# The first modulation vectors of a two-block network: all on VectorE, or slice by slice on VectorE and TensorE

## The reference, cut to what matters

```python
c_act = jax.nn.silu(c)
mod = (c_act @ w_ada[l] + b_ada[l])[:, None, :]
sh1, sc1, gt1, sh2, sc2, gt2 = jnp.split(mod, 6, axis=-1)
h = rms_norm(x, g_mix[l]) * (1.0 + sc1) + sh1
x = x + gt1 * token_mix(h, w_in[l], ...)       # first step inside: z = h @ w_in
```

## Time and profile before

| | us |
|---|---|
| runs of the kernel | 2795.12, 2797.88, 2808.26 |
| median | 2797.88 |
| profiled execution: span from first to last instruction | 2800.8 |
| TensorE busy in it | 2691.0 (96%) |
| VectorE busy | 1985.4 (71%) |
| ScalarE busy | 1455.6 (52%) |
| GpSimd busy | 123.4 (4%) |
| mean granted TensorE clock | 0.986 of full speed |

### The profile page before, as it was taken

One profiled execution on the slowest core, in us unless ns is written; L12 is line 12 of the kernel. 1 busy time (PEld: TensorE's weight loads), 2 busy tenths in 40 slices (PEclk: granted clock), 3 DMA queues, 4 the chain that ended last, 5 costly groups with the idle time before them and its releaser, 6 DMA issues.

```text
span 2800.8 us, 45758 instructions
## 1 busy us (share of the span) xinstructions
PE 2691.0 (96%) x15906; PEld 2311.4 (83%) x15906; DVE 1985.4 (71%) x2871; ACT 1455.6 (52%) x2187; POOL 123.4 (4%) x72
## 2 busy tenths in 40 slices
PE   5999899998999989999999999999999999999999
PEld 3866678885999867888799987999877888799987
DVE  7754689996998566653699847899455753699954
ACT  3353478885555246753555525555236753455532
POOL 1532111100000000000000000000000000000000
PEclk9999799998999999999999999999999999999999
DMA  7631499993332231123233232322232123223222
GB/s 284 273 135 38 169 345 408 406 367 121 106 105 91 90 144 67 52 76 113 83 106 105 90 113 83 104 103 94 90 112 99 60 68 113 98 91 105 90 98 98
DMA packets 95244, 377.57 MB, mean 135 GB/s; under 512 B 10832, under 2 KB 11104, under 8 KB 92896
## 3 DMA queue, kind: packets, MB, share of 16 engines
q1 hardware_dynamic: 89072, 348.69, 34.5%
q0 software_dynamic: 4608, 16.78, 1.5%
q10 hardware_dynamic: 1456, 10.66, 0.9%
HBM read 363.50 MB, written 16.78 MB: 136 GB/s over the span
## 4 chain that ended last, share of the span: by engine, by line
PE 83%; DVE 7%; issue 5%; ACT 4%; DMA 0%; POOL 0%; SPq 0%; ACTq 0%; DVEq 0%; POOLq 0%
PE pb L1402 15%; PE pb L1404 15%; PE pb L1403 15%; PE pb L1787 10%; PE pb L1789 10%; PE pb L1788 10%; PE pb L1971 1%; PE pb L2003 1%; PE pb L1927 1%; PE pb L1476 1%; DVE g_wl L2507 1%; ACT SP L1284 1%; DVE hid L2686 1%; PE pb L1655 1%; PE pb L1980 0%
## 5 line engine op out<-in xcount | busy, mean ns | idle before, releaser
L1787 PE MATMUL pb<-bl,g_wh 128*128 128x256 f32 x2464 | 701.7, 285 | 14.7 <-DVE bl L2597 5.7
L1789 PE MATMUL pb<-bh,g_wh 128*128 128x256 f32 x2464 | 697.9, 283 | 0.0
L1788 PE MATMUL pb<-bh,g_wl 128*128 128x256 f32 x2464 | 697.9, 283 | 0.0
L1787 PEld LDWEIGHTS pb<-bl,g_wh 128*128 128x128 f32 x2464 | 473.5, 192 | 20.1 <-issue 8.4
L1788 PEld LDWEIGHTS pb<-bh,g_wl 128*128 128x128 f32 x2464 | 473.7, 192 | 1.6 <-issue 1.4
L1789 PEld LDWEIGHTS pb<-bh,g_wh 128*128 128x128 f32 x2464 | 473.6, 192 | 0.0
L2636 DVE TENSOR_TENSOR w_lo<-raw,w_hi 128x1024 fp32r<-128x1024 f32 x164 | 200.3, 1223 | 203.1 <-ACT w_hi L679 202.3
L1402 PE MATMUL pb<-hl,w_hi 128*128 128x512 f32 (+1 forms) x728 | 303.1, 416 | 23.4 <-DVE hl L2131 10.2
L679 ACT ACTIVATE w_hi<-raw 128x1024 fp32r<-128x1024 f32 x194 | 204.2, 1057 | 195.2 <-PE pb L1404 181.6
L1404 PE MATMUL pb<-hh,w_hi 128*128 128x512 f32 (+1 forms) x728 | 286.0, 393 | 0.0
L1403 PE MATMUL pb<-hh,w_lo 128*128 128x512 f32 (+1 forms) x728 | 285.9, 393 | 0.0
(11 more groups left out here) (450 smaller groups left out, 5364.1 us busy)
## 6 DMA issues: line engine op xcount, KB each, us to landing
raw<-in_wstream SPq DMA_DIRECT2D x220, 512.0 KB, 3.2
m_raw<-in_moe_stream SPq DMA_DIRECT2D x96, 512.0 KB, 6.0
g_own<-in_gu_stream SPq DMA_DIRECT2D x44, 768.0 KB, 4.0
raw<-in_gu_stream SPq DMA_DIRECT2D x44, 768.0 KB, 4.1
m_first<-in_moe_stream SPq DMA_DIRECT2D x48, 512.0 KB, 6.0
hf<-in_moe_stream SPq DMA_DIRECT2D x48, 512.0 KB
ada_ring<-in_ada SPq DMA_DIRECT2D x8, 2048.0 KB, 8.1
g_own<-in_gu_stream SPq DMA_DIRECT2D x44, 256.0 KB, 2.9
```

What stands on the lines that cost most here:

```text
L1787: pe.matmul(o, lh, rl, start=first and k == 0, stop=False, skip_group_check=True)
L1788: pe.matmul(o, ll, rh, start=False, stop=False, skip_group_check=True)
L1789: m = pe.matmul(o, lh, rh, start=False, stop=k == 3, skip_group_check=True)
```

## The change

The first vectors are made in eight steps, one for each slice of 128 features.

- The host stores the first 16 output slices of ada in pairs (scale slice k, shift slice k), and c by partitions in vec. SP issues crow, x in two halves, pair 0 (1 MB), two weight chunks, pairs 1 to 7.
- ScalarE's queue issues con first, then vec, lvec. ScalarE waits for crow and vec, makes silu of both forms of c and two small values, then squares x and makes the root, and only then makes the high halves of the first two weight chunks. Their low halves go from VectorE to POOL.
- The shift of a slice is made by TensorE: 8 matmuls with 128 x 128 of ada as weights and one moving column of silu(c) (`shift`), into banks that are not used yet. ScalarE adds the bias. The scale stays with VectorE (8 passes), and its gain is formed for each slice alone.
- Norm and products follow each slice. TensorE's order is: shift of slice k, product of slice k-2 for the first z tile, of slice k-3 for the second.
- TensorE runs two matmuls on con before the sums of squares.
- The ring loads of ada wait for all gains and for all shifts.
- Semaphores are reused, which moves some constants in waits.

```diff
@@ SyncE
         def _(sp):
             sp.dma_start(crow[:], bass.AP(cond.tensor, 0, [[0, P], [1, D]])).then_inc(x_in, 16)
-            def load_first_ada(d):
-                cols = slice(ADA_EACH * d, ADA_EACH * (d + 1))
-                sp.dma_start(adaw[:, cols, :], ada[:, cols, :]).then_inc(ada_in[d], 16)
+            def load_first_ada(k):
+                sp.dma_start(adaw[:, 2 * k:2 * k + 2, :], ada[:, 2 * k:2 * k + 2, :]).then_inc(first_in[k], 16)
+            sp.dma_start(x[:, 0:4, :], xT[:, 0:4, :]).then_inc(x_half, 16)
+            sp.dma_start(x[:, 4:KD, :], xT[:, 4:KD, :]).then_inc(vec_in, 16)
             load_first_ada(0)
             for s in range(2):
                 sp.dma_start(raw[s][:], wstream[s]).then_inc(w_raw[s], 16)
-            sp.dma_start(x[:], xT).then_inc(vec_in, 16)
-            for d in range(1, ADA1 // ADA_EACH):
-                load_first_ada(d)
+            for k in range(1, KD):
+                load_first_ada(k)
             def stream_pair(j, g_done=None):
                 for s in range(2):
...
                              ada[:, bass.ds(ADA1 + ADA_EACH * d, ADA_EACH), :]).then_inc(ada_in[u], 16)
             stream_pair(1)
-            sp.wait_ge(mod_ready, 1)
+            sp.wait_ge(mod_ready, 2 * KD)
+            sp.wait_ge(shift_or_ov_c_mm, KD)
             for u in range(2):
                 load_ada(u, u)
             with sp.Fori(1, (ADA - ADA1) // ADA_EACH // 2) as i:
@@ GpSimd
                                        V("conv_w", n, w).unsqueeze(2).broadcast_to([P, w, P]), ALU.mult).then_inc(diag_ready, 1)
             j0 = C_WOUT // 2 - 3
+            for s in range(2):
+                pool.wait_ge(w_hid, s + 1)
+                pool.tensor_tensor(w_lo[s][:], raw[s][:], w_hi[s][:].bitcast(F32), ALU.subtract).then_inc(w_lod, 1)
             lows(1, j0)
             low(j0, 0)
             pool.wait_ge(con_in, 16)
-            pool.wait_ge(vec_in, 48)
+            pool.wait_ge(x_in, 32)
             pool.wait_ge(ada_used, (ADA - ADA1) // ADA_EACH)
             low(j0, 1)
             for i, (j, s) in enumerate(((j0 + 1, 0), (j0 + 1, 1), (j0 + 2, 0))):
@@ ScalarE
         @block.scalar
         def _(act):
-            act.dma_start(vec[:], vecs).then_inc(vec_in, 16)
+            act.dma_start(con[:], const).then_inc(con_in, 16)
+            act.dma_start(vec[:], vecs).then_inc(x_in, 16)
             act.dma_start(lvec_all[:], lvecs.rearrange("l p n -> p l n")).then_inc(vec_in, 16)
-            act.dma_start(con[:], const).then_inc(con_in, 16)
             for started in (*z_evac, m_silu, vT_ready):
                 act.sem_inc(started, 1)
             step = Tally(act, astep)
...
                         act.activation(hh[:, k, :], htmp[:, k % 2, :], ACT.Identity,
                                        bias=shift(k)).then_inc(h_hi, 1)
-            act.wait_ge(x_in, 16)
+            act.wait_ge(x_in, 32)
             act.activation(crow[:], crow[:], ACT.Silu).then_inc(c_act, 1)
-            for s in range(2):
-                hi(0, s, used=False)
-            act.wait_ge(vec_in, 48)
+            act.activation(c_col, V("cond", 0, KD), ACT.Silu).then_inc(c_act, 1)
             step(act.activation(small[:, 8:8 + NR], V("lam", 0, NR), ACT.Abs))
             act.activation(small[:, 12:12 + NR], small[:, 8:8 + NR], ACT.Exp, scale=-1.0).then_inc(c_act, 1)
             act.preload_act_table_set(LN_EXP)
-            squares(0, lambda k: None)
+            for k in range(KD):
+                act.wait_ge(*((x_half, 16) if k < 4 else (vec_in, 32)))
+                square(0, k, sq_ring)
             norm_root(0)
+            for s in range(2):
+                hi(0, s, used=False)
             act.dma_start(lruw[:], lru_gates).then_inc(mixer_in, 16)
             act.dma_start(glaw[:], gla_gate).then_inc(mixer_in, 16)
             act.dma_start(scm[:], masks).then_inc(mixer_in, 16)
-            act.wait_ge(mod_ready, 1)
-            norm_hi(0, 0, None, shift=lambda k: modv[:, 8 + k:9 + k])
+            for k in range(KD):
+                act.wait_ge(shift_or_ov_c_mm, k + 1)
+                step(act.activation(modv[:, KD + k:KD + k + 1], shift_of(k), ACT.Identity, bias=V("b_ada", KD + k)))
+                act.wait_ge(h_tmp, k + 1)
+                act.activation(hh[:, k, :], htmp[:, k % 2, :], ACT.Identity, bias=modv[:, KD + k:KD + k + 1]).then_inc(h_hi, 1)
             for j in range(NZ // 2):
@@ TensorE
                 pe.sem_inc(started, 1)
             pe.sem_inc(g_used, 7)
             pe.wait_ge(con_in, 16)
+            for _ in range(2):
+                pe.matmul(pb[1][:], ident, con[:, 0:T], start=True, stop=True)
             stats(0)
...
                 pe.wait_ge(z_evac[s], 1 + j)
                 proj(pb[1 + s][:], s)
-            for s in range(2):
-                chunk(C_WIN // 2, s)
-                pe.wait_ge(z_evac[s], 1)
-            both_along_norm(0, 5)
+            def shift(k):
+                if k == 0:
+                    pe.wait_ge(c_act, 2)
+                pe.wait_ge(first_in[k], 16)
+                for i in range(KD):
+                    m = pe.matmul(shift_of(k), adaw[:, 2 * k + 1, i * P:(i + 1) * P], c_col[:, i:i + 1], start=i == 0, stop=i == KD - 1)
+                m.then_inc(shift_or_ov_c_mm, 1)
+            def first_z(s, k):
+                if k == 0:
+                    chunk(C_WIN // 2, s)
+                    pe.wait_ge(z_evac[s], 1)
+                pe.wait_ge(h_ready, k + 1)
+                m = mm3(pb[1 + s][:], w_hi[s][:, k, :], w_lo[s][:, k, :], hh[:, k, :], hl[:, k, :], k == 0, k == KD - 1)
+                if k == KD - 1:
+                    m.then_inc(w_used, 1)
+            for k in range(KD + 3):
+                if k < KD:
+                    shift(k)
+                if 2 <= k < KD + 2:
+                    first_z(0, k - 2)
+                if k >= 3:
+                    first_z(1, k - 3)
             with pe.Fori(1, NZ // 2) as j:
                 for s in range(2):
                     z_tile(j, s)
@@ VectorE
                 return dve.scalar_tensor_tensor(w, w, 1.0, crow[:], ALU.mult, ALU.mult, accum_out=to)
+            dve.wait_ge(x_in, 32)
+            step(dve.tensor_scalar(gain_from, V("b_ada", 0, KD), 1.0, None, ALU.add))
             dve.wait_ge(c_act, 1)
-            for i in range(ADA1):
-                if i % ADA_EACH == 0:
-                    dve.wait_ge(ada_in[i // ADA_EACH], 16)
-                ins = modulate(adaw[:, i, :], modv[:, i:i + 1])
-                if i == ADA_EACH - 1:
-                    for s in range(2):
-                        dve.wait_ge(w_hid, s + 1)
-                        dve.tensor_tensor(w_lo[s][:], raw[s][:], w_hi[s][:].bitcast(F32), ALU.subtract).then_inc(w_lod, 1)
-            step(ins)
-            dve.wait_ge(vec_in, 48)
-            step(dve.tensor_tensor(modv[:, 0:ADA1], modv[:, 0:ADA1], V("b_ada", 0, ADA1), ALU.add))
-            dve.scalar_tensor_tensor(gs[:, 0, :], modv[:, 0:8], 1.0, V("g_mix", 0, KD), ALU.add, ALU.mult).then_inc(mod_ready, 1)
-            dve.wait_ge(mod_ready, 1)
-            norm_h(0, 0, lambda k: gs[:, 0, k:k + 1], lambda k: modv[:, 8 + k:9 + k])
-            dve.wait_ge(c_act, 2)
+            def first_low(k):
+                dve.wait_ge(h_hi, k + 1)
+                dve.scalar_tensor_tensor(hl[:, k, :], htmp[:, k % 2, :], modv[:, KD + k:KD + k + 1], hh[:, k, :].bitcast(F32),
+                                         ALU.add, ALU.subtract).then_inc(h_ready, 1)
+            for k in range(KD):
+                dve.wait_ge(first_in[k], 16)
+                modulate(adaw[:, 2 * k, :], modv[:, k:k + 1]).then_inc(mod_ready, 1)
+                dve.wait_ge(mod_ready, 2 * k + 1)
+                dve.tensor_scalar(gs[:, 0, k:k + 1], modv[:, k:k + 1], gain_from[:, k:k + 1], V("g_mix", k), ALU.add, ALU.mult
+                                  ).then_inc(mod_ready, 1)
+                if k == 0:
+                    dve.wait_ge(rs_ready, 1)
+                    dve.wait_ge(vec_in, 32)
+                if k >= 2:
+                    dve.wait_ge(h_ready, k - 1)
+                dve.wait_ge(mod_ready, 2 * k + 2)
+                dve.scalar_tensor_tensor(htmp[:, k % 2, :], x[:, k, :], gs[:, 0, k:k + 1], rs[:], ALU.mult, ALU.mult).then_inc(h_tmp, 1)
+                if k >= 1:
+                    first_low(k - 1)
+            first_low(KD - 1)
+            dve.wait_ge(c_act, 3)
             e1, tt_, t2, po = (small[:, c:c + NR] for c in (12, 16, 20, 36))
             step(dve.tensor_scalar(tt_, e1, 2.0, None, ALU.add))
             step(dve.reciprocal(tt_, tt_))
@@ host
     ada_c = col_chunks(ada)
     order = [1, 0, 2, 4, 3, 5]
     ada_c = np.concatenate([ada_c[8 * n:8 * n + 8] for n in order])
+    first = np.stack([ada_c[:KD].transpose(3, 0, 2, 1), ada_c[KD:ADA1].transpose(1, 0, 2, 3)], axis=2).reshape(P, ADA1, D)
+    ada_all = np.concatenate([first, ada_c[ADA1:].transpose(3, 0, 2, 1).reshape(P, ADA - ADA1, D)], axis=1)
```

(26 more changed lines are left out.)

## The result

The changed kernel takes 2830.35 us (median of 5 runs, 2829.49 to 2833.23), the kernel before 2797.88 (2795.12 to 2808.26): ratio 1.0109, 95% interval 1.0095 to 1.0123. It is slower, as the forecast said, but by 32 us (by the medians; 30.5 by the ratio) and not by 8; the time lies outside the range. The profiled execution has a span of 2829.0 us, 28.2 more than that of before. In all the profiled runs whose time is listed the span is 1.8 to 1.9 us shorter than the time, so the profiled execution of before took about 2802.7 (an estimate), 5 us over its median: a difference of spans against this one profile comes out a few us smaller than a difference of times.

A forecast was written before the change was run, and what follows sets the result against it. VectorE was taken to bound the opening, transfers close behind. Third tile 10.2 us later, less 1.5 us of a later wait, gave +8.7 on 2797.88: 2806.6, rounded to 2806, range 2792 to 2812.

The forecast's parts named there:

- new constants in waits and 8 KB instead of 16 per partition in a transfer: all nothing: Side effects of the diff: changed wait constants and a smaller transfer were priced at nothing.
- My own sign for being wrong: Behind the opening: the forecast is wrong if more than 3 us move after 170 us.
- Root at 23.3: ScalarE in the opening: the norm's root was to come at 23.3 us instead of 34.8.
- POOL holds VectorE, 4.4 us: Opening: POOL's first two low halves each hold up a VectorE instruction, 2 x 2.2 = 4.4 us.
- Clock 0.50 from 28 to 60: TensorE in the opening: granted clock of 0.50 (1.2 GHz) from about 28 to 60 us.
- A shift at 3.44 slow and 1.8 fast: TensorE: one slice's 8 shift matmuls take 3.44 us at the slow clock, 1.8 at the fast.
- Last wait of tile three: Before the third z tile: its weights need ScalarE's 1.14 and POOL's 2.39 us after tile one.
- Sum of the opening: Net of the opening: third tile 10.2 us later, 1.5 us of a later wait gone, +8.7 us.
- A: Opening: TensorE's clock stays fast, VectorE bounds, third tile at 55.0, 2796 us; chance 0.2.
- B: Opening: as A, and POOL doesn't hold VectorE, 4.4 us less, 2791 us; chance 0.05.
- C: Late start: vec lands near 12 to 14, all shifts by 5 us, 2812; decided by landing after 9; chance 0.1.
- D: Opening: TensorE's clock rises between slices and falls again, +3 us, 2801; chance 0.15.

The follow-up runs named there:

- e1: Kernel before with 8 unused columns (32 bytes a partition) after vec, nothing else changed: 2824.26 us, ratio 1.0082.
- e6: Changed kernel with c by partitions in unused columns of small, by its own transfer, so every buffer keeps its old place: 2807.81 us, ratio 1.0039.
- e11: As e7, small transfer first on ScalarE's queue, first high halves made earlier on ScalarE, low halves on VectorE instead of POOL: 2803.54 us, ratio 1.0016.
- e5: Kernel before with 8 unused columns ahead of x, so every buffer moves 32 bytes and no distance changes: 2798.24 us, ratio 1.0002.
- e12: Changed kernel with 120 unused columns after vec, 64 bytes ahead of ysb, two unused matmuls after each of shifts 0 to 2: 2793.64 us, ratio 0.9976.
- e4: Changed kernel with 24 unused columns after vec, two unused 512-column matmuls after each of shifts 0 to 2, one after 3 to 7: 2823.53 us, ratio 1.0091.
- e7: As e6, with two unused 512-column matmuls after each of shifts 0 to 2: 2802.11 us, ratio 1.0014.
- e8: As e6, first halves made earlier, second z tile four slices behind the shifts, one unused matmul after shifts 0 to 2: 2813.00 us, ratio 1.0057.
- e9: Kernel before with 16 unused columns (64 bytes) ahead of ysb, moving the experts' m_hi and m_lo but not gh: 2793.30 us, ratio 0.9978.
- e3: Kernel before with 16 unused columns (64 bytes) after vec: 2806.97 us, ratio 1.0025.

## Why the prediction was wrong

**The step that failed** is the one that priced "new constants in waits and 8 KB instead of 16 per partition in a transfer: all nothing", and with it "equal durations behind it". The edit that made most of the loss was not even in that list: eight columns more in vec. I costed instructions, waits and transfers, and no edit for where it puts the buffers behind it. e1 prices it by itself at 20.6 us of span (0.0082 of 2798, 22.9 us, by the runs), and e6 takes it out and leaves 1.0039, 10.9 us, where I had forecast 8.7 (with a later start and an earlier rise of the clock that partly cancel). My own sign for being wrong, more than 3 us moving after 170 us, came true with 19.7.

Point by point, the opening:

- Root at 23.3: it was at 24.97. The first square was at 12.92 and not 11.5, since the late vec (8.84) and two table loads stand before it. The squares to root took 12.05 us, not 11.8: no gain from the two early matmuls of con.
- POOL holds VectorE, 4.4 us: 2.40 and 2.83 instead of 0.75 each, 3.7 us. The mechanism was there and, by the trace, on the path: TensorE's 3.70 idle us before the first product end with the held `hl`. No run takes the holds alone out of the changed kernel; e11, where they are off the path, has unused matmuls in that gap.
- First product near 30: 32.54. ScalarE's and VectorE's order before it was right, each step later by the root's 1.7 and by the holds.
- Clock 0.50 from 28 to 60: it fell at 28.8 and was back at 52.7, so the last two shifts and the tail were fast. The third tile came at 64.64 and not at 67.4 although the first product was 2.5 us later. So the early rise gave back 2.8 + 2.5 = 5.3 us (an estimate from these times), and the near hit on this tile is in part luck: two errors that offset each other.
- A shift at 3.44 slow and 1.8 fast: 3.41 and 1.84. A slow slice 6.0: 39.93 to 45.90, 5.97. The rows of 128x4 matmuls were the right neighbours for one column.
- Last wait of tile three, of which high and low half were to take 1.14 + 2.39 = 3.5: its high half began at 61.02 and the tile at 64.64, 3.6.
- Ring loads near 59: 57.41. The wait of 1.9 us is gone: between 57 and 180 TensorE waits once for POOL, 2.3 us, for tile three itself.
- Sum of the opening: +8.7. At 170 us it is +8.5, but in another mix: +7.4 for the tile, -1.9 for the wait, and about +3 already from the wider spacing in the z tiles. The 1.9 is of the one profile of before, and by e5 the place at 170 is only good to some 2 us.

The rivals. A and B did not happen. Where the clock is held, e12 comes near A: its third tile is at 55.86, against A's 55.0. e4 (60.88) and e7 (58.84) are later by more, but e4 has the wide spacing and five more unused matmuls, and e7 starts at 11.58 instead of 8.84. A had its number nearly right for another reason: I had let VectorE bound this case, and in e12 as in e11 it is TensorE, which begins no shift before the statistics end and then has no idle moment until its tiles do, in part with unused work. C has its place (vec late) at a small price: it landed at 8.84, just under its deciding point of 9. D is half there, in the clock's rise at 52.7.

Of the clock: the stretch 334 to 338 had told rightly that busy time does not hold it. The Trainium skill, "TensorE: Matmul & The Clock Gate", "Why this matters for your kernels", asks that TensorE be kept busy without a break and have no long idle gap between bursts. By that rule alone the clock would have come back in the 15 busy microseconds from 35 to 50; the trace disagrees, and e8, where it fell within a busy stretch, disagrees more plainly.

That distance sets the spacing is shown by e1, e5, e9 and e12. Why is open: the runs give no rule beyond "a multiple of 512 is fast", with 32, 64 and 128 off slower by 6.6, 0 to 5 and 5.5 ns. At 64 off the experts lose 6.4; their 64 are short of a multiple where those of e3 are past it, and no run tells whether that makes the difference.

## What to carry to other kernels

When a diff changes the size of any buffer, list the new addresses of all buffers behind it, and the distances between the operands of the commonest matmuls; an edit outside the loops can cost or give every matmul in them a few ns. If the time behind a change moves evenly, compare the mean of one instruction, group by group, before looking for waits. Moving vector work to thin matmuls on TensorE can also take its clock away, as it did here: price them at both levels, together with the wide products that stand between them. And before two kernels are compared at one place of their profiles, compare two profiles of the same instructions: here they differed by 2 us.

## What the runs showed of the hardware

- Back to back at the full clock, 512-column matmuls start 0.2267 us apart when the distance between the stationary and the moving buffer is a multiple of 512 bytes in a partition (in the kernel before, in e9 for the experts, and in e12 at 512 more), and 0.2333 apart at 32 bytes off. At 128 off it is 0.2322, at 64 off 0.226 to 0.233 by the pair. Moving every buffer by 32 bytes changed nothing (226 to 228 ns in e5). The 256-column products of g_wh stayed at 283 ns on the mean, but no run changed the distance between their operands.
- Matmuls with one moving column, eight of 128x128 weights in 16 instructions, take 3.41 us at 1.2 GHz and 1.84 at 2.4; with four columns it is 3.58 and 1.93. A TensorE kept busy with them and three products a slice fell to 1.2 GHz without an idle moment (39.4 in e8); two unused 512-column matmuls after each of the first three shifts kept it at 2.4 (e7).
- While POOL made a low half, VectorE's instructions took 2.40 and 2.83 us instead of 0.75, and POOL's own 2.92 instead of 2.35.
- After one wait of about 2 us near 80 us the clock fell to 1.2 GHz for 3.4 us in the profiles of e3, e5 and e9 and not in that of the kernel before: 1.7 to 1.8 us of difference between equal instructions.
